# Moving the operand parts hh, hl, fh and fl to other residues in SBUF, in a two-part float32r matmul kernel

## The chip, the cores and the metric

The kernel runs on one core of one Trainium2 chip (trn2). The metric is the device time of one execution, in microseconds; the median of several executions is compared.

## The reference

The reference computes two transformer-like blocks on 256 positions of 1,024 features, batch 1. Cut to its matrix products:

```python
# first block
mod = silu(c) @ w_ada + b_ada                      # 6 modulation vectors
proj = (layer_norm(x) * (1 + sc1) + sh1) @ w_in    # 1024 -> 4096
ya = silu(layer_norm(causal_dwconv31(a_val * sigmoid(a_gate)))) @ w_pw_a
yb = einsum(pooled, w_pool) * pool_scale
x = layer_norm(ALPHA * x + g1 * ((sigmoid(gate_a) * ya + sigmoid(gate_b) * yb) @ w_out))
h = layer_norm(x) * (1 + sc2) + sh2
v, gt = split(causal_dwconv3(h @ w_up))            # 1024 -> 2 * 2816
x = layer_norm(ALPHA * x + g2 * ((gelu(gt) * v) @ w_down))
...
# second block, two layers: gated delta rule (w_in, w_out), SwiGLU (w13, w2),
#                           block attention (w_qkv, w_out), SwiGLU (w13, w2)
```

All of it is float32. The products with the large weights are more than nine tenths of the work.

## The kernel before, in words

The weights are cut into 311 units of 128 x 1,024 float32 (512 KB each), plus 48 units of `w_ada`, in the fixed order of a list, `PLAN`. SyncE's DMA queue loads them one after another into a ring `raw` of 11 slots. ScalarE rounds a unit to float32r into `hi` (line 1005, five slots), VectorE computes `lo = raw - hi` as float32r (line 1472, five slots), and the activations are split in the same way into `hh` and `hl` (8 chunks of 128 x 256 each) and, for the feed-forward stages, into `fh` and `fl` (4 chunks each). VectorE also does the 48 units of `w_ada` (line 1459).

TensorE then computes each product as three float32r matmuls, `hi*hh + hi*hl + lo*hh`, in the helper `three` (line 509), which nearly all matmuls go through. In `tile`, `first_tiles` and `rows_in` the weights' part is the stationary operand (128 columns) and the activations' part the moving one (256 columns); in `z` (the gate of the delta rule) and `rows_out_of` (the last feed-forward stage) the roles are exchanged, and the moving operand has 512 columns of weights. A matmul on the profile's page stands as `ps<-moving,stationary`: `ps<-hh,hi` streams `hh` past `hi`. Each matmul loads its stationary operand anew (a row of LDWEIGHTS), also where two in a row use the same one. Line 504 (`spin`) issues matmuls on a constant tile `idle` that no result uses. Lines 516 and 528 (`norm`) and line 607 (`conv`, the convolution over 31 positions) multiply plain float32; each of these stands as two records in the trace. `conv` reads its moving operand from `ypad` at element 2 + i for tap i, so from tap 12 on it starts 56, 60, 64, ... 128 bytes past a multiple of 128.

Each engine runs its own program in the order in which it is written; semaphores join them. The order of instructions and of waits is fixed in the source. SBUF tensors are placed one after another in the order of their `sb(...)` calls. Their first bytes in each partition are, in the build of before: `raw` 2,048, `hi` 47,104, `lo` 67,584, `hh` 88,064, `hl` 96,256, `fh` 104,448, `fl` 108,544, `idle` 112,640, `crow` 113,664, `xa` 117,760, `h` 125,952, `B0` 134,144 to `ev` 185,344, `Z` 189,440, `sm` 214,016, `blk` 215,040, `ones` 217,088: all of these are multiples of 1,024. `cst` starts at 218,624 and `vec` at 225,536 (both 512 past a multiple of 1,024), `mod` at 228,192. Within a unit, stationary tiles start every 512 bytes, and moving tiles of `hh` every 1,024.

Of the kernel before, what the change touches and what calls it, by code (L numbers as in the profile page):

```python
# [13 lines left out]
P = 128  # L14
# [277 lines left out]
def program(nc, wts, head, vecs, csts, rows, xtok, xT, low_dram, inv_dram, out):  # L292
    with ExitStack() as ctx:
        def sb(name, shape, dt=F):
            return ctx.enter_context(nc.sbuf_tensor(name, shape, dt))
# [2 lines left out]
            return ctx.enter_context(nc.semaphore(name))  # L298


        first = sb("first", [P, 184])
        dummy = sb("dumm", [P, 16])
        eps = sb("eps", [P, 24])
        raw = sb("raw", [P, RAW, 1024])
        hi = sb("hi", [P, SPLIT, 1024], FR)
        lo = sb("lo", [P, SPLIT, 1024], FR)
        hh = sb("hh", [P, NC, S], FR)
        hl = sb("hl", [P, NC, S], FR)
        fh = sb("fh", [P, 4, S], FR)
        fl = sb("fl", [P, 4, S], FR)  # L310
        idle = sb("idle", [P, S], FR)
# [7 lines left out]
        ypad = Z[:, 0:4 * 288].rearrange("p (g s) -> p g s", g=4)  # L319
        sm = sb("sm", [P, 256])  # L320
        blk = sb("blk", [64, 2, 256])
        ones = sb("ones", [P, 3, P])
        cst = sb("cst", [P, NCST])
        vec = sb("vec", [P, NVEC])
        mod = sb("mod", [P, 48])
        bank = [ctx.enter_context(nc.psum_tensor(f"ps{i}", [P, 512], F)) for i in range(8)]

        def V(name, i=0, n=1):
# [1872 lines left out]
```

## Time and profile before

| | |
|---|---|
| median of 3 runs | 1187.76 us (1185.19 to 1189.2) |
| the profiled execution, its own time | 1187.91 us |
| its span, first to last instruction | 1186.1 us |
| TensorE busy (matmuls) | 1129.2 us, 95% |
| VectorE busy | 808.1 us, 68% |
| ScalarE busy | 615.0 us, 52% |
| mean granted TensorE clock | 0.982 of full |
| moved by DMA | 195.60 MB, mean 165 GB/s |

The span lies 1.8 us below the execution's own time. Durations of matmuls in the rows contain the way through the array, and successive matmuls overlap, so the pace of TensorE is read from the starts in the timeline, not from the mean duration of one.

### The profile page before, as it was taken

The page shows a single profiled execution, that of the slowest core. Times are in us where ns is not written, and L with a number is a line of the kernel's source. Part 1 is how long each engine was busy: PE and PEld are TensorE (multiplying, and loading weights), DVE is VectorE, ACT ScalarE, POOL GpSimd, SP SyncE. Part 2 cuts the span into 40 slices and gives each one's busy share as a digit, 9 for nine tenths or more (in the row PEclk, how much of TensorE's full clock was granted, in tenths as well). Part 3 has the DMA queues.
Part 4 walks back from the last instruction along what each step waited for, and adds up shares of the span by engine and source line. Part 5 has one row for each costly group of instructions (what it writes and reads, how often), then busy time and mean ns, then how long its engine had stood idle before and what let it go on. Part 6 is the DMA issues. An engine that isn't in the chain of part 4 may idle for free.

```text
span 1186.1 us, 20553 instructions
## 1 busy us (share of the span) xinstructions
PE 1129.2 (95%) x8544; PEld 1090.4 (92%) x8544; DVE 808.1 (68%) x1360; ACT 615.0 (52%) x1028; POOL 3.3 (0%) x13
## 2 busy tenths in 40 slices
PE   7999989999999998879989999999999999999997
PEld 7998888899999997679989999999999799999996
DVE  7987479878877786585766755555589647555555
ACT  5567444556465548733443644444455545545453
POOL 0000000000000000000000000000000000000000
PEclk9999999999999998989989999999999999999999
DMA  9984237356766513133223265555435342655520
GB/s 376 419 313 160 72 142 273 100 183 227 243 209 205 187 65 122 46 100 140 90 72 125 90 197 192 178 182 177 159 116 193 120 141 82 220 193 180 187 80 36
DMA packets 58557, 195.60 MB, mean 165 GB/s; under 512 B 10848, under 2 KB 11232, under 8 KB 58208
## 3 DMA queue, kind: packets, MB, share of 16 engines
q1 hardware_dynamic: 58464, 194.28, 48.1%
q8 instruction: 68, 1.11, 0.4%
q14 instruction: 25, 0.20, 0.1%
HBM read 192.94 MB, written 1.31 MB: 164 GB/s over the span
## 4 chain that ended last, share of the span: by engine, by line
PE 76%; DVE 14%; ACT 6%; issue 2%; DMA 1%; SPq 1%; DVEq 0%; ACTq 0%
PE ps L509 64%; DVE lo L1472 3%; PE ps L722 3%; PE ps L516 2%; ACT hi L1005 2%; PE ps L607 2%; DVE raw L1459 1%; DVE B L1481 1%; PE ps L528 1%; DVE st L1489 1%; DVE B L1785 1%; DVE B L1494 1%; DVE ev L1710 1%; DVE B L1594 1%; SPq L477 1%
## 5 line engine op out<-in xcount | busy, mean ns | idle before, releaser
L509 PE MATMUL ps<-hh,hi 128*128 128x256 f32 x1792 | 515.9, 288 | 13.2 <-DVE hl L1506 3.4
L509 PE MATMUL ps<-hl,hi 128*128 128x256 f32 x1792 | 509.6, 284 | 0.0
L509 PE MATMUL ps<-hh,lo 128*128 128x256 f32 x1792 | 509.5, 284 | 0.0
L1472 DVE TENSOR_TENSOR lo<-raw,hi 128x1024 fp32r<-128x1024 f32 x311 | 378.2, 1222 | 179.3 <-ACT hi L1005 178.5
L509 PEld LDWEIGHTS ps<-hh,hi 128*128 128x128 f32 x1792 | 346.4, 193 | 16.9 <-issue 6.6
L1005 ACT ACTIVATE hi<-raw 128x1024 fp32r<-128x1024 f32 x311 | 324.0, 1050 | 55.8 <-PE ps L509 55.4
L509 PEld LDWEIGHTS ps<-hl,hi 128*128 128x128 f32 x1792 | 346.5, 193 | 1.0
L509 PEld LDWEIGHTS ps<-hh,lo 128*128 128x128 f32 x1792 | 346.3, 193 | 0.0
L509 PE MATMUL ps<-fh,hi 128*128 128x256 f32 x392 | 113.1, 289 | 4.0 <-ACT B L1109 2.7
L509 PE MATMUL ps<-fl,hi 128*128 128x256 f32 x392 | 112.1, 286 | 0.0
L509 PE MATMUL ps<-fh,lo 128*128 128x256 f32 x392 | 112.1, 286 | 0.0
L1166 ACT ACTIVATE ev<-ps 128x256 f32<-128x256 f32 x88 | 33.6, 382 | 132.9 <-PE ps L509 132.9
L509 PEld LDWEIGHTS ps<-fh,hi 128*128 128x128 f32 x392 | 76.4, 195 | 4.7 <-ACT B L1109 3.3
L509 PEld LDWEIGHTS ps<-fl,hi 128*128 128x128 f32 x392 | 76.6, 195 | 0.0
L509 PEld LDWEIGHTS ps<-fh,lo 128*128 128x128 f32 x392 | 76.5, 195 | 0.0
L1459 DVE CUSTOM_DVE_ANT_0 raw<-raw,crow 128x1024 f32<-128x1024 f32 x48 | 58.3, 1219 | 0.0
L504 PE MATMUL ps<-idle 128*128 128x256 f32 x404 | 55.3, 295 | 1.7 <-POOL Z L494 1.7
L1717 DVE TENSOR_TENSOR ev<-ev 128x256 f32<-128x256 f32 x66 | 28.1, 426 | 42.2 <-ACT ev L1166 31.5
L504 PEld LDWEIGHTS ps<-idle 128*128 128x128 f32 x404 | 51.9, 196 | 2.5 <-POOL Z L494 1.7
L1719 DVE TENSOR_TENSOR fl<-ev,fh 128x256 fp32r<-128x256 f32 x66 | 28.1, 425 | 31.9 <-ACT fh L1170 31.9
L1785 DVE SCALAR_TENSOR_TENSOR B<-ps,vec,B 128x255 f32<-128x255 f32 (+2 forms) x72 | 34.6, 481 | 22.0 <-ACT B L1255 20.3
L1170 ACT ACTIVATE fh<-ev 128x256 fp32r<-128x256 f32 x66 | 27.6, 418 | 35.9 <-DVE ev L1717 35.9
(256 smaller groups left out, 1223.7 us busy)
## 6 DMA issues: line engine op xcount, KB each, us to landing
raw<-in_w SPq DMA_DIRECT2D x359, 512.0 KB, 4.0
B<-in_t SPq DMA_DIRECT2D x2, 512.0 KB, 5.0
xa<-in_x SPq DMA_DIRECT2D x1, 1024.0 KB, 10.4
B<-in_r SPq DMA_DIRECT2D x1, 1024.0 KB, 6.2
out<-h SPq DMA_DIRECT2D x4, 256.0 KB, 2.0
cst<-in_c SPq DMA_DIRECT2D x1, 864.0 KB, 8.5
B<-between SPq DMA_DIRECT2D x32, 4.0 KB, 1.6
vec<-in_v SPq DMA_DIRECT2D x1, 328.5 KB, 6.7
```

The costliest lines, as they stand in the source:

```text
L504: g.matmul(bank[7][:, 0:S], idle[:, 0:P], idle[:, :], start=True, stop=True, skip_group_check=True)
L509: m = g.matmul(o, l, r, start=first and n == 0, stop=last and n == 2, skip_group_check=True)
L516: m = g.matmul(bank[bm][:, 0:S], ones[:, one, :], y[:, k, :], start=k == 0, stop=k == nch - 1, skip_group_check=True)
L722: m = g.matmul(bank[b][:, i * P:i * P + P], left(i), right(i), start=i == 0, stop=True, skip_group_check=True)
L1005: g.activation(hi[:, j % SPLIT, :], raw[:, PLACE[j] % RAW, :], ACT.Copy).then_inc(*up("hi", j))
L1166: g.activation(e, p, ACT.Copy if half else ACT.Silu).then_inc(*up("ff_out", (kup, t)))
L1170: g.activation(fh[:, j % 4, :], ev[:, (2 * j) % 4, :], ACT.Copy).then_inc(*up("f_hi", (kup, j)))
L1459: g.tensor_tensor_reduce(r, r, crow[:, :], 1.0, 0.0, ALU.mult, ALU.add, mod[:, col:col + 1]).then_inc(*up("ada", n))
L1472: g.tensor_tensor(lo[:, j % SPLIT, :], raw[:, PLACE[j] % RAW, :], hi[:, j % SPLIT, :].bitcast(F), ALU.subtract).then_inc(*up("lo", j))
L1717: g.tensor_tensor(e0, e0, e1, ALU.mult).then_inc(*up("f", (kup, j)))
L1719: g.tensor_tensor(fl[:, j % 4, :], e0, fh[:, j % 4, :].bitcast(F), ALU.subtract).then_inc(*up("f_lo", (kup, j)))
L1785: m = g.scalar_tensor_tensor(out=dst[:, d:], in0=bank[b][:, 0:S - d], scalar=V("a_conv", t * 4 + i), in1=dst[:, d:], op0=ALU.mult, op1=ALU ...
```

## The change

Only the places of SBUF tensors change. `mod` (192 bytes per partition) and `ones` (1,536 bytes) are allocated ahead of `hh` instead of at the end, an unused tensor `gap0` of 96 bytes follows them, and an unused `gap1` of 32 bytes stands between `hl` and `fh`.

```diff
         hi = sb("hi", [P, SPLIT, 1024], FR)
         lo = sb("lo", [P, SPLIT, 1024], FR)
+        mod = sb("mod", [P, 48])
+        ones = sb("ones", [P, 3, P])
+        gap0 = sb("gap0", [P, 24])
         hh = sb("hh", [P, NC, S], FR)
         hl = sb("hl", [P, NC, S], FR)
+        gap1 = sb("gap1", [P, 8])
         fh = sb("fh", [P, 4, S], FR)
         fl = sb("fl", [P, 4, S], FR)
         idle = sb("idle", [P, S], FR)
...
         blk = sb("blk", [64, 2, 256])
-        ones = sb("ones", [P, 3, P])
         cst = sb("cst", [P, NCST])
         vec = sb("vec", [P, NVEC])
-        mod = sb("mod", [P, 48])
```

In the build of the change, `raw`, `hi` and `lo` stay where they were. `mod` starts at 88,064, `ones` at 88,256 (64 bytes past a multiple of 128), `hh` at 89,888 and `hl` at 98,080 (both 32 past one), `fh` at 106,304 and `fl` at 110,400 (64 past one). Everything behind them up to `blk` moves up by 1,856 bytes and is then 64 past a multiple of 128: `idle` 114,496, `xa` 119,616, `B0` 136,000, `Z` 191,296 and so on. `cst` (218,944) and `vec` (225,856) move up by 320 bytes. No instruction is added, removed or moved on any engine, no wait changes, and every operand keeps its shape, type and strides.

## Rows read from the trace of the kernel before

**Rows 1.** The page: span, and busy time by engine.

```profile
span 1186.1 us, 20553 instructions
PE 1129.2 (95%) x8544; PEld 1090.4 (92%) x8544; DVE 808.1 (68%) x1360; ACT 615.0 (52%) x1028; POOL 3.3 (0%) x13
```

**Rows 2.** The page: the chain that ended last, by engine.

```profile
PE 76%; DVE 14%; ACT 6%; issue 2%; DMA 1%; SPq 1%; DVEq 0%; ACTq 0%
```

**Rows 3.** The chain from 640 to 910 us, one piece: start, us, what.

```profile
661.03 187.47 PE ps L509 x1560
```

**Rows 4.** Groups of matmuls (moving, stationary): count, busy us, mean ns, idle before.

```profile
L509 PE MATMUL ps<-hh,hi 128*128 128x256 f32 x1792 | 515.9, 288 | 13.2 <-DVE hl L1506 3.4
L509 PE MATMUL ps<-fh,hi 128*128 128x256 f32 x392 | 113.1, 289 | 4.0 <-ACT B L1109 2.7
L504 PE MATMUL ps<-idle 128*128 128x256 f32 x404 | 55.3, 295 | 1.7 <-POOL Z L494 1.7
L509 PE MATMUL ps<-hi,fh 128*128 128x512 f32 x88 | 34.5, 392 | 0.0
L509 PE MATMUL ps<-hi,hh 128*128 128x512 f32 x64 | 27.0, 422 | 0.0
```

**Rows 5.** Timeline of TensorE at full clock: start us, duration us, operands.

```profile
1019.57 0.28 PE L509 MATMUL ps<-hl,hi 128*128 128x256 f32 x1
...
1021.49 0.28 PE L509 MATMUL ps<-hh,lo 128*128 128x256 f32 x1
```

**Rows 6.** Timeline of TensorE at half clock, and that stretch's granted clock.

```profile
17.15 0.41 PE L509 MATMUL ps<-hl,hi 128*128 128x256 f32 x1
...
18.43 0.41 PE L509 MATMUL ps<-hl,hi 128*128 128x256 f32 x1
...
16.30:19.60 3.30, 2.80 (x13) 0.50 1.02 418
```

**Rows 7.** Timeline of TensorE: plain float32 of taps 12 and 14; one record's duration.

```profile
69.97 1.89 PE L607 MATMUL ps<-Z,B 128*128 128x256 f32 x8
79.18 1.89 PE L607 MATMUL ps<-Z,B 128*128 128x256 f32 x8
L607 PE MATMUL ps<-Z,B x152: 377/378/532, 70.0 to 139.2; 128*128 128x256 f32 x152
```

**Rows 8.** Timeline of TensorE: after a change of kind, and further on.

```profile
1008.21 0.40 PE L509 MATMUL ps<-hi,fh 128*128 128x512 f32 x1
1009.14 0.39 PE L509 MATMUL ps<-hi,fl 128*128 128x512 f32 x1
...
1010.96 0.28 PE L509 MATMUL ps<-hh,hi 128*128 128x256 f32 x1
1011.07 0.28 PE L509 MATMUL ps<-hl,hi 128*128 128x256 f32 x1
1171.55 0.39 PE L509 MATMUL ps<-lo,fh 128*128 128x512 f32 x1
...
1175.40 0.39 PE L509 MATMUL ps<-hi,fl 128*128 128x512 f32 x1
```

**Rows 9.** One tile's matmuls (hh): ns minimum, median, maximum.

```profile
L509 PE MATMUL ps<-hh,hi x1792: 277/283/562, 16.8 to 1169.4; 128*128 128x256 f32 x200
```

**Rows 10.** Groups of VectorE by form: shifted by 4 bytes, and in line.

```profile
L1594 DVE SCALAR_TENSOR_TENSOR B<-Z,vec,B 128x256 f32<-128x256 f32 x44 | 18.3, 478 | 0.0
L1530 DVE SCALAR_TENSOR_TENSOR xa<-ps,mod,B 128x256 f32<-128x256 f32 x16 | 6.4, 475 | 0.0
```

**Rows 11.** DMA issues: count, KB each, median us to landing.

```profile
raw<-in_w SPq DMA_DIRECT2D x359, 512.0 KB, 4.0
xa<-in_x SPq DMA_DIRECT2D x1, 1024.0 KB, 10.4
```

**Rows 12.** The chain from 210 to 420 us, shares by line.

```profile
by line: PE ps L509 63.1%; DVE lo L1472 10.6%; ACT hi L1005 3.9%; DVE raw L1459 3.8%; DVE ev L1710 3.3%; PE ps L516 2.9%; DVE ev L1707 2.7%; DVE B L1481 2.1%; issue 1.8%; DVE ev L1717 1.5%; ACT ev L1164 1.4%; DVE st L1489 0.8%; DVE h L1499 
```

**Rows 13.** Windows: us, busy us of VectorE, granted clock, DMA share, GB/s.

```profile
661.00:848.00 187.00, 103.43 (x124) 1.00 0.55 179
```

## The prediction

> **What bounds the kernel now.** I read the page's busy shares first. TensorE is at work in 95% of the span, VectorE in 68%, ScalarE in 52% [rows 1]. The chain of waits says the same of the end: three quarters of it are TensorE's [rows 2], and one piece of it is 1,560 matmuls of line 509 without a break, 187.47 us, or 120.2 ns each [rows 3]. So the time of this kernel is a number of matmuls times their pace, plus short serial stretches around the norms.
>
> The number comes from the groups. The three products with `hh` and `hl` moving are 1,792 each and the three with `fh` and `fl` 392 each: 6,552 matmuls of 256 columns; with the roles exchanged there are 3 x 88 + 3 x 64 = 456 of 512 columns [rows 4]. The 404 on `idle` fill waits and I leave them out. The clock was 0.982 of full in the mean; halved clock in 3.6% of the span is 43 us, or at most 200 matmuls. About 6,350 + 456 = 6,800 matmuls at full clock are left, so **each nanosecond per matmul is worth 6.8 us**, and 0.3% of the time, 3.6 us, is 0.5 ns per matmul.
>
> The pace comes from starts in the timeline. At full clock 16 successive matmuls take 1.92 us, 120.0 ns each [rows 5]. At half clock six take 1.28 us, 213.3 ns [rows 6]: that is 256 columns at 1.2 GHz and nothing else. At 2.4 GHz 256 columns are 106.7 ns, so 13.3 ns per matmul is something other than columns. Plain float32 does not have most of it: eight records of `conv` take 1.89 us from the first start to the last end, less 0.378 for the last one's duration, over seven, is 216 ns [rows 7], 2.7 over the 213.3 of its slower stream. With 512 columns the float32r matmul settles at 3.85 us for 17, 226.5 ns [rows 8], again 13.2 over 213.3. So the excess belongs to each float32r matmul with its load and not to its columns, and it is there only when the stream runs at the full rate. Its size is not fixed either: the first four of 512 columns after a change of kind take 0.93 us, 232.5 ns each, and the first of 256 behind them takes 0.11 us [rows 8]. The matmul's own duration goes from 277 ns to the usual 283 [rows 9]. This looks like the load of the next stationary operand and the moving stream getting in each other's way, in a rhythm that depends on how they stand in time. Whether it also depends on where they stand in memory is the whole question of this change.
>
> **The change part by part.** No instruction, wait or transfer is added or removed, so there is no term of the form "so many of these". Four things could have a price.
>
> 1. Moving operands 32 (`hh`, `hl`) or 64 (`fh`, `fl`) bytes past a multiple of 128, stationary ones unmoved: this touches all 6,800. In the trace of before every float32r operand starts at a multiple of 512, so no row varies what the change varies. Two things speak for zero. First, the pace is the same 120 whatever the distance of the two operands is in large steps: within a unit the weights' tile advances by 512 bytes and the moving tile by 1,024, through five slots, and the piece of rows 3 stays at 120.2 throughout. Second, the only operands that do vary in small steps cost nothing: tap 12 of `conv` reads its moving operand 56 bytes past a multiple of 128 and tap 14 64 past it, and eight records take 1.89 us both times [rows 7]. What weakens this: `conv` streams at half the rate and has none of the excess, so it has slack in which a collision would not be seen. Bounds: down to the 110 ns of the one fast start [rows 8], −10 ns; up to the 6 ns by which the slow starts of 512 columns lie over the settled pace. I take 0, since the nearest row with a small shift shows 0.
>
> The Trainium skill (TensorE: Matmul & The Clock Gate, Step-by-step: what each phase is for) says that TensorE has two independent SBUF read ports and that loading the next weights does not steal bandwidth from the running matmul. By that rule placement could not matter: this term would be 0, neither rival below would have a chance, and 3.6 us to both sides would do for the range. But the same page (Wait — 56ns, not 53.3ns?) gives a fixed 2.5 ns over the columns, where this trace has 13.3 for float32r and 2.7 for plain float32. The trace has room for a conflict of the two reads that the page excludes, so I keep both rivals.
>
> 2. Stationary `hh` and `fh`, moving `hi` and `lo` (456 matmuls, in `z` and `rows_out_of`): same question with the roles exchanged, already in the 6,800. Alone it would be worth at most 456 x 10 ns = 4.6 us.
>
> 3. VectorE and ScalarE operands 32 or 64 bytes off. The taps of line 1594, which read at 4-byte shifts, take 478 ns; line 1530, the same form on operands in line, takes 475 [rows 10]. Three nanoseconds on the 1,360 − 311 instructions that touch a moved tensor are 3.1 us, of which the chain carries 14%: 0.4 us. I take 0. The 311 of `lo` touch unmoved tensors alone.
>
> 4. Transfers. The 359 loads of weights go to unmoved slots; only a few land in moved tensors, such as `xa` in 10.4 us [rows 11]. They lie beside the weights' stream; the two of `in_t` at the start could delay the first norm. A fifth on a 5 us transfer is 1 us. I take 0.
>
> **The sum** is 1187.91 us, the profiled execution's own time (its span is 1186.1), plus 0. The median of the runs is 1187.76, 0.15 us lower, so I forecast 1187.8, with a range of its own of 3.6 us to both sides; 0.3% is also about the least that a measurement of this kernel can tell from no change.
>
> **The rivals.**
>
> *The excess shrinks* (the operands collided because both start on the same residue, and no longer do). For it: 13.3 ns is a large excess, it comes only with two full-rate reads, it varies by how they meet, and before, all three families of tensors stand on the same residue, after it on three different ones. Against it: rows 7. Price: what the excess loses. TensorE does not get all of it. In the first feed-forward stage, 210 to 420 us, only 63% of the chain is line 509 and the rest mostly VectorE's `lo` and `raw` [rows 12]; 210 us hold about 1,690 matmuls, and 37% of them, some 600, would gain nothing. Elsewhere there is room: in the piece of rows 3 VectorE is busy in 103 of 187 us [rows 13], so a pace of 110 leaves it under 61%. That leaves 6,200 matmuls. If half of the 10.6 ns over plain float32 goes, that is 5.3 x 6,200 = 33 us, 1155 us; if all, 66 us, 1122. The weights would still arrive: 24 matmuls at 110 ns are 2.64 us per 512 KB.
>
> *The excess grows*: the rhythm in which the pair has settled is a good one, and with the stream 32 bytes ahead of the load they meet as they do in the slow starts. It comes at each of the 6,800 matmuls, and nothing hides it, since TensorE is the bound. At the +6 ns of rows 8 that is 41 us, 1229 us. It decides from +0.5 ns per matmul on. Against it: the slow starts settle within four to six matmuls of themselves.
>
> That the change does not do what it says can be left out: the addresses of the build are 702 x 128 + 32 for `hh` and 830 x 128 + 64 for `fh`, and the instructions are the same.
>
> **How the numbers follow.** No change 0.42, because the only shifted rows show none; the excess shrinks 0.38, because something does collide and the change parts what stood on one residue; the excess grows 0.20, by the slow starts. The time is that of the first, 1187.8. The range must hold 8 times in 10, over both signs: from 1130, which leaves out the last part of a full gain (about 0.07), to 1203, which holds an excess grown by up to 2.2 ns and leaves out 0.12.
>
> **What the profile would show.** If I am right, the timeline has 120.0 ns between starts in every stage, and the long piece of the chain stays at 187 us. If the excess shrinks, starts stand 109 to 119 apart, the median duration of the `hh` matmuls falls from 283 towards 277, the piece of rows 3 falls below 185 us, and the first feed-forward stage gains the least. If it grows, starts of 256 columns stand 121 to 126 apart. A different pace for `fh` than for `hh` would say that the residue itself counts (64 against 32), a different pace with `hi` than with `lo` that the distance does. A changed VectorE or transfer time with the pace at 120 would make step 3 or 4 wrong.

## The result

The change is faster by 1.3%: 1170.92 us in the median of its four runs (1169.08 to 1176.3) against 1187.41, a ratio of 0.9869 with a 95% interval of 0.983 to 0.9909. The profiled execution took 1169.08 us with a span of 1167.3, 18.8 us below the span of before. So the forecast of no change was wrong; the time lies inside the range, on the side of the first rival.

The page after the change; line numbers are 3 higher than before, so line 512 is the helper `three`.

```profile
span 1167.3 us, 20553 instructions
PE 1109.0 (95%) x8544; PEld 1068.4 (92%) x8544; DVE 807.5 (69%) x1360; ACT 614.9 (53%) x1028; POOL 3.3 (0%) x13
...
PE 73%; DVE 17%; ACT 7%; issue 2%; SPq 1%; DMA 0%; POOL 0%; ACTq 0%; DVEq 0%; POOLq 0%
...
L512 PE MATMUL ps<-hh,hi 128*128 128x256 f32 x1792 | 511.2, 285 | 15.2 <-DVE hl L1509 3.5
...
L512 PE MATMUL ps<-fh,hi 128*128 128x256 f32 x392 | 109.9, 280 | 3.9 <-ACT B L1112 2.9
...
L507 PE MATMUL ps<-idle 128*128 128x256 f32 x404 | 55.3, 295 | 1.7 <-POOL Z L497 1.7
```

Against [rows 1] only TensorE's busy time has moved, by 20 us; VectorE and ScalarE are busy for as long as before. Within TensorE, the mean duration of the matmuls with `hh` and `fh` moving has fallen, 288 to 285 ns and 289 to 280, and that of `idle`, whose moving and stationary operand are the same tile, is 295 as before [rows 4].

The pace is in the timeline and in the long piece of the chain. Columns: start us, duration us, operands.

```profile
1011.10 0.28 PE L512 MATMUL ps<-hl,hi 128*128 128x256 f32 x1
...
1012.97 0.28 PE L512 MATMUL ps<-hh,lo 128*128 128x256 f32 x1
1155.66 0.39 PE L512 MATMUL ps<-hi,fh 128*128 128x512 f32 x1
...
1158.93 0.39 PE L512 MATMUL ps<-lo,fh 128*128 128x512 f32 x1
```

Sixteen matmuls of 256 columns take 1.87 us, 116.9 ns each, where [rows 5] had 120.0. Fourteen of 512 columns with exchanged roles take 3.27 us, 233.6 ns each, where [rows 8] settled at 226.5: these have become slower. The piece of 1,560 matmuls [rows 3] is here:

```profile
653.15 181.27 PE ps L512 x1560
```

It is 6.20 us shorter, 4.0 ns per matmul. I took the mean distance between starts over the whole trace as well, leaving out distances that hold a wait or a half-clock stretch: 117.04 ns for `hh` and `hl` (119.89 before, 5,224 and 5,250 matmuls), 115.42 for `fh` and `fl` (119.97, 1,155 and 1,134), 232.7 for 512 columns (228.9), 119.55 for `idle` (119.55). 5,224 x 2.85 = 14.9 us and 1,155 x 4.55 = 5.3 us less, 439 x 3.8 = 1.7 us more: the paces give 18.5 us, and the spans differ by 18.8.

That the two agree to 0.3 us is partly luck. The profiled execution after the change had 33.2 us of its span at half clock, the one before 43.5 (mean granted clocks 0.986 and 0.982). At 213.3 ns in place of 120 per matmul [rows 5, 6], 10.3 us less at half clock are worth up to 4.5 us, by my estimate. Against that, one stage kept only 2.0 us of what its pace would give, as shown below. The medians differ by 16.5 us.

### The profile page after: what moved, and what is told of

It is laid out like the page before. It is cut to its first block, busy times and chain, and to the rows that moved or that the text cites. A ratio compares the mean times of both kernels' runs of the same rounds, so it can differ in the third digit from the quotient of the medians.

```text
span 1167.3 us, 20553 instructions
## 1 busy us (share of the span) xinstructions
PE 1109.0 (95%) x8544; PEld 1068.4 (92%) x8544; DVE 807.5 (69%) x1360; ACT 614.9 (53%) x1028; POOL 3.3 (0%) x13
## 4 chain that ended last, share of the span: by engine, by line
PE 73%; DVE 17%; ACT 7%; issue 2%; SPq 1%; DMA 0%; POOL 0%; ACTq 0%; DVEq 0%; POOLq 0%
PE ps L512 61%; DVE lo L1475 4%; PE ps L725 3%; ACT hi L1008 2%; DVE raw L1462 2%; PE ps L610 2%; PE ps L519 2%; DVE B L1484 1%; PE ps L531 1%; DVE ev L1713 1%; DVE st L1492 1%; PE ps L507 1%; DVE ev L1710 1%; DVE B L1788 1%; DVE B L1497 1%
## 5 line engine op out<-in xcount | busy, mean ns | idle before, releaser
L512 PE MATMUL ps<-hh,lo 128*128 128x256 f32 x1792 | 504.3, 281 | 0.0
L512 PE MATMUL ps<-hl,hi 128*128 128x256 f32 x1792 | 503.9, 281 | 0.0
L512 PEld LDWEIGHTS ps<-hh,hi 128*128 128x128 f32 x1792 | 340.7, 190 | 19.9 <-issue 9.6
L512 PEld LDWEIGHTS ps<-hl,hi 128*128 128x128 f32 x1792 | 340.6, 190 | 1.1
L512 PEld LDWEIGHTS ps<-hh,lo 128*128 128x128 f32 x1792 | 340.7, 190 | 0.0
L512 PE MATMUL ps<-fh,hi 128*128 128x256 f32 x392 | 109.9, 280 | 3.9 <-ACT B L1112 2.9
L512 PE MATMUL ps<-fh,lo 128*128 128x256 f32 x392 | 108.8, 278 | 0.0
L512 PE MATMUL ps<-fl,hi 128*128 128x256 f32 x392 | 108.8, 277 | 0.0
L512 PEld LDWEIGHTS ps<-fl,hi 128*128 128x128 f32 x392 | 73.6, 188 | 0.0
```

The costliest lines, as they stand in the source:

```text
L512: m = g.matmul(o, l, r, start=first and n == 0, stop=last and n == 2, skip_group_check=True)
```

## The experiments

The theory after this result, called the pair theory below: the read of the moving operand and the load of the next stationary one collide, and how often depends on the distance of the two operands' addresses (the start of the moving one minus the start of the stationary one). The rivals: the moving operand's own residue counts, not the distance; or it was another moved tensor (`idle` and those behind it, most of which VectorE, ScalarE and the transfers use).

### One part of the change at a time

Only `hh` and `hl` 32 bytes past a multiple of 128 (h32_only):

```diff
+        gap0 = sb("gap0", [P, 8])
         hh = sb("hh", [P, NC, S], FR)
         hl = sb("hl", [P, NC, S], FR)
+        gap1 = sb("gap1", [P, 24])
         fh = sb("fh", [P, 4, S], FR)
```

> Only hh and hl move, to 32 bytes past a multiple of 128; fh, fl and everything behind are on multiples of 128. Pair theory: the 5,250 matmuls at full clock go from 119.9 to about 117.0 ns (less 15 us, a little of it lost where VectorE bounds), the 192 of 512 columns get 4 ns slower (plus 0.8 us): 1173 to 1175 us. If the tensors behind were the cause: 1187.

Measured: 1172.25 us, ratio 0.9864 (0.9847 to 0.9881): within 1 us of what was expected, and all of the gain of the change. `hh` runs at 116.81 ns. Unexpected: `fh`, at residue 0, runs at 118.62 and not at 120.

Only `fh` and `fl` at 64 (f64_only):

```diff
+        gap1 = sb("gap1", [P, 16])
         fh = sb("fh", [P, 4, S], FR)
         fl = sb("fl", [P, 4, S], FR)
+        gap2 = sb("gap2", [P, 16])
         idle = sb("idle", [P, S], FR)
```

> Only fh and fl move, to 64 bytes past a multiple of 128; everything behind them is back on multiples of 128. Pair theory: the 1,176 matmuls on them go from 120.0 to about 115.4 ns (less 5 us), the 264 of 512 columns from 228.8 to 232.4 (plus 1 us): 1183 to 1185 us. If the tensors behind were the cause: 1187.

Measured: 1188.94 us, ratio 0.9997 (0.9978 to 1.0016). A miss: `fh` came down only to 117.74 ns, not to the 115.4 that it has in the change, and the 512 columns went up to 233.7 ns, 4.9 more. 1,132 x 2.2 = 2.5 us less and 263 x 4.9 = 1.3 us more is a gain of 1.2 us, within what the runs can tell. So the pace of `fh` also depends on what `hh`, in the tiles between, leaves behind. The traces say more: `fh` at distance 64 has two paces. In the change it ran at 113.7 ns in the first SwiGLU of the second block and at 116.9 in the first feed-forward stage; in f64_only it ran at 117.9 in both. The pairs below show both, 113.3 and 117.8, at that distance.

Only what lies behind (behind_only):

```diff
         fl = sb("fl", [P, 4, S], FR)
+        gap2 = sb("gap2", [P, 16])
         idle = sb("idle", [P, S], FR)
```

> hh, hl, fh and fl stay; idle and everything behind it move to 64 bytes past a multiple of 128. Pair theory: nothing, 1187 us. If the operands of VectorE, ScalarE or the transfers were what counts: most of the 16 us of the change, 1171 us.

Measured: 1189.56 us, ratio 1.0009 (0.9996 to 1.0022). No pace moved (`hh` 119.89, `fh` 119.97 ns). The theory of another tensor falls.

The same piece of the chain in h32_only, f64_only and behind_only, in this order, one fence each:

```profile
651.59 183.27 PE ps L511 x1560
```
```profile
661.58 186.49 PE ps L511 x1560
```
```profile
660.48 187.48 PE ps L510 x1560
```

### The distance by itself

Three programs with nothing but matmuls on constants measure the pace of pairs of residues. Each was executed once. Below, 0/32 means the stationary operand 0 bytes in and the moving one 32. Each line is a run of 96 (or 48) in the order of `three` (the code is shortened):

```python
w(p, k, r) = wt[:, p * 4096 + k * 128 + r // 4 : ... + 128]   # stationary, r bytes in
m(q, k, r) = mv[:, q * 4096 + k * 256 + r // 4 : ... + 256]   # moving, r bytes in
[mm(bank[t][:, 0:S], w(p, k, a), m(q, k, b)) for t in range(4) for k in range(8) for p, q in THREE]
```

> A program that does none of the reference's work: constants in two tensors and, line by line, runs of 96 float32r matmuls of 256 columns (or 48 of 512) in the order of the helper three, each line with another pair of residues of the stationary and the moving operand; it copies x to the output. Pair theory (the excess depends on the residue of the moving operand relative to the stationary one): the pace of 256 columns is 120 ns at equal residues, also at 32/32 and 64/64, and about 117 and 115.5 at 0/32 and 0/64. Absolute theory (the moving operand's own residue counts): 32/32 gives 117 and 64/64 115.5, and moving the stationary operand alone does nothing. With 512 columns 226.7 at equal residues and about 233 at 32 or 64 apart.

In m1_pairs the lines went through one helper, so they are read by windows of 10 us, each within one line. Columns: window, its length and TensorE's busy us, matmuls that touch it (those under way at its start count too), granted clock, DMA. In this order (stationary/moving): 0/0, 0/4, 0/32, 0/64, 0/256, 64/0, 32/32, 64/64, 32/96.

```profile
24.00:34.00 10.00, 10.00 (x86) 1.00 0.01 2
36.00:46.00 10.00, 10.00 (x83) 1.00 0.01 2
70.00:80.00 10.00, 10.00 (x88) 1.00 0.01 2
92.00:102.00 10.00, 10.00 (x87) 1.00 0.01 2
183.00:193.00 10.00, 10.00 (x85) 1.00 0.01 2
240.00:250.00 10.00, 10.00 (x90) 1.00 0.00 0
274.00:284.00 10.00, 10.00 (x86) 1.00 0.01 2
286.00:296.00 10.00, 10.00 (x86) 1.00 0.00 0
319.00:329.00 10.00, 10.00 (x91) 1.00 0.01 2
```

By the starts, in the second half of each line: 0/0, 32/32, 64/64 and 0/256 exactly 120.0 ns; 0/4 123.3; 0/32 116.7; 0/64 117.8 (a miss, I expected 115.5); 64/0 and 32/96 113.3. With 512 columns 226.7 at 0/0, 32/32 and 64/64, and 233.4 at 32/0. The moving operand's own residue does not set the pace, since 32/32 and 64/64 are as 0/0: the absolute theory falls. The pair theory stands, with exceptions: 0/64 and 32/96 are both 64 apart and differ, and two more follow below.

> The same kind of program as m1_pairs, none of the reference's work: for each distance of 16 to 240 bytes of the moving operand from the stationary one, 96 matmuls of 256 columns behind 48 at distance 0, and again 96 behind 48 at distance 192. If the distance alone sets the pace: the same pace in both, with 113.3 ns at 112 and 192 as in m1_pairs. If the rhythm that was there before also counts (m1_pairs had 117.8 ns at 0/64 and 113.3 at 32/96, both 64 apart): two paces at some distances. If the pattern repeats after 128 bytes: 240 like 112 and 192 like 64. With 512 columns and the roles exchanged: 226.7 at 0 and 229 to 234 elsewhere.

In m2_residues each line is one group. Distances 16, 32, 64, 112, 128, 192 and 240 behind a run at distance 0 (columns: start, duration of the 96, line):

```profile
29.95 11.56 PE L67 MATMUL ps<-mv,wt 128*128 128x256 f32 x96
...
64.15 11.47 PE L71 MATMUL ps<-mv,wt 128*128 128x256 f32 x96
...
80.92 11.36 PE L73 MATMUL ps<-mv,wt 128*128 128x256 f32 x96
...
131.99 11.47 PE L79 MATMUL ps<-mv,wt 128*128 128x256 f32 x96
...
234.33 11.10 PE L91 MATMUL ps<-mv,wt 128*128 128x256 f32 x96
...
250.71 11.12 PE L93 MATMUL ps<-mv,wt 128*128 128x256 f32 x96
...
267.42 11.55 PE L95 MATMUL ps<-mv,wt 128*128 128x256 f32 x96
...
403.75 11.06 PE L111 MATMUL ps<-mv,wt 128*128 128x256 f32 x96
...
504.94 11.41 PE L123 MATMUL ps<-mv,wt 128*128 128x256 f32 x96
```

Lines 73 and 93 are distances 32 and 112 once more, behind a run at 192. Paces in the second half of each line (where there are two, the first is behind a run at 0, the second behind one at 192): 118.7 at 16 (116.7 in m1_pairs), 117.8 or 116.7 at 32, 118.3 at 48, 117.8 at 64, 120.1 or 118.4 at 80, 119.9 at 96, **113.3 at 112 in both**, 118.6 at 128, 118.8 or 118.6 at 144, 117.3 or 118.6 at 160, 119.2 at 176, 113.3 at 192, 119.1 at 208, 118.3 at 224, 117.1 at 240. So 240 is not as 112 and 128 not as 0: the pattern does not repeat after 128 bytes. 64 and 192 do not tell, since both have been seen at 113.3 and at 117.8. And some distances have two paces, by what ran before. The two runs of 48 at distance 192, one behind distance 16 and one behind 32:

```profile
41.35 5.82 PE L68 MATMUL ps<-mv,wt 128*128 128x256 f32 x48
...
75.47 5.62 PE L72 MATMUL ps<-mv,wt 128*128 128x256 f32 x48
```

The first settled at 117.8 ns, the second at 113.3, with nothing else different. With 512 columns and the stationary operand 176, 192 and 240 bytes in: 229.7, 228.9 and 226.7 ns, and 232.2 to 233.4 at the others of this program except 0 (in m1_pairs, 228.8 at 0/64, 230.7 at 8/0 and 234.3 at 96/0).

> None of the reference's work, as m1_pairs. (1) Pairs 112 bytes apart mod 256 (0/112, 0/368, 32/144, 64/176, 144/0 as stationary/moving): if the distance mod 256 sets the pace, 113.3 ns in the first four and in 0/1136 and 0/368, and 144/0 as well, since it is -144 = 112. (2) 72 matmuls on one and the same pair at distances 0 to 240: if the two reads of one matmul and the next load collide, the same distances matter as with changing operands; if it were the change of slots, 120 at every distance. (3) Plain float32, which streams at half the rate, at distances 0 to 192: if the excess is a collision of reads that needs the full rate, 216 ns per record at every distance.

Of m3_kinds three groups of 72 on one and the same pair at distances 0, 4 and 64 (lines 81, 82, 84), and three of plain float32, 48 records each, at distances 0, 4 and 112 (lines 89, 90, 93):

```profile
147.08 8.80 PE L81 MATMUL ps<-mv,wt 128*128 128x256 f32 x72
155.72 9.03 PE L82 MATMUL ps<-mv,wt 128*128 128x256 f32 x72
...
172.99 8.33 PE L84 MATMUL ps<-mv,wt 128*128 128x256 f32 x72
...
214.49 10.52 PE L89 MATMUL ps<-mv,wt 128*128 128x256 f32 x48
224.84 10.54 PE L90 MATMUL ps<-mv,wt 128*128 128x256 f32 x48
...
255.94 10.52 PE L93 MATMUL ps<-mv,wt 128*128 128x256 f32 x48
```

The same pair again and again has the same dependence (120.0, 123.4 and 113.3 ns), so the change of slots is not needed for it. Plain float32 has none: 216 ns per record at every distance. 0/112, 0/368, 0/1136, 32/144 and 64/176 all settled at 113.3, so whole multiples of 256 bytes do not count, nor does a common shift of 32 or 64. One miss: 144/0, which is -144 = 112 mod 256, settled at 118.3. Both lines below stand behind a run at 0/0, first 0/112, then 144/0:

```profile
29.90 11.10 PE L67 MATMUL ps<-mv,wt 128*128 128x256 f32 x96
...
79.96 11.52 PE L73 MATMUL ps<-mv,wt 128*128 128x256 f32 x96
```

m1_pairs has two more like it: 96/0 ran at 120.0 ns, where 0/160, the same distance mod 256, had 117.3 and 118.6, and 16/0 ran at 118.3, where 0/240 had 117.1. In all three the stationary operand is the one that is moved; 32/0, 64/0 and 128/0 agree with their distance. So the distance orders most pairs but is not all that counts. Whether these three are further rhythms of their distances, or the place of the stationary operand counts by itself, was not tried.

### The distances in the kernel

The same map, put into the kernel. All four tensors 4 bytes (1 element) in, which the pairs make slower (all4b), and 112 bytes (28 elements) in (all112):

```diff
-        hh = sb("hh", [P, NC, S], FR)
-        hl = sb("hl", [P, NC, S], FR)
-        fh = sb("fh", [P, 4, S], FR)
-        fl = sb("fl", [P, 4, S], FR)
+        hx = sb("hx", [P, 2 * NC * S + 64], FR)
+        fx = sb("fx", [P, 2 * 4 * S + 64], FR)
+        hh, hl = (hx[:, 28 + i * NC * S:28 + (i + 1) * NC * S].rearrange("p (c s) -> p c s", c=NC) for i in (0, 1))
+        fh, fl = (fx[:, 28 + i * 4 * S:28 + (i + 1) * 4 * S].rearrange("p (c s) -> p c s", c=4) for i in (0, 1))
```

> hh, hl, fh and fl 4 bytes past a multiple of 256, everything behind on multiples of 256. m1_pairs had 123.3 ns there, 3.3 above the 120 of equal residues: 3.3 ns x 6,350 = 21 us more, and 456 x 4 ns = 2 us: 1210 us, slower than before. If the misplacement of an operand only ever helps, or its lines do not matter: 1170 to 1188.

Measured: 1204.86 us, ratio 1.0135 (1.0114 to 1.0155), slower by 16 us; `hx` at 123.12 ns, `fx` at 123.24. The direction and the pace are as expected, the time is 5 us short of it. These executions had mean clocks of 0.982 to 0.985, those of before beside them 0.975 to 0.982. Over the 42 executions of before on record the time falls by some 0.74 us for each 0.001 of mean clock (a line through them, my estimate), so the clock may well be the missing 5 us.

> hh, hl, fh and fl 112 bytes past a multiple of 256 (a multiple of 16, not of 32), everything behind on multiples of 256. In m2_residues this distance went to 113.3 ns whatever ran before it, where 192 had two rhythms, 113.3 and 117.8. Pair theory: 6.6 ns x 5,800 = 38 us less and 456 x 5 ns = 2 us more: 1151 to 1155 us, with less spread between executions than all192 (1154 to 1170). If 112 is as unsteady in the real order: 1155 to 1170.

Measured: 1160.45 us, ratio 0.9766 (0.9749 to 0.9783), four runs within 1159.41 to 1161.8; `hx` at 114.16 ns, `fx` at 113.50. The pace is within 1 ns of the expected one, the time 5 to 9 us above, inside the range that was given for an unsteady 112. The pieces of the chain of all4b and all112:

```profile
669.39 192.66 PE ps L509 x1560
```
```profile
651.47 177.13 PE ps L509 x1560
```

Two more put all four tensors 192 or 64 bytes past a multiple of 256 with a `gap0` ahead of `hh` and the rest of 256 ahead of `idle`:

```diff
+        gap0 = sb("gap0", [P, 48])
         hh = sb("hh", [P, NC, S], FR)
...
+        gap2 = sb("gap2", [P, 16])
         idle = sb("idle", [P, S], FR)
```

> hh, hl, fh and fl 192 bytes past a multiple of 256, the weights' parts and everything behind on multiples of 256. Pair theory with the pace of m1_pairs at 192: 113.3 ns in place of 120 for the 6,400 matmuls of 256 columns at full clock, less 6.6 ns x 5,800 (some 600 gain nothing in the first feed-forward stage) = 38 us, plus 456 x 5 ns = 2 us: 1152 us. If the real order of slots and chunks does not settle in the fast rhythm: about 117 ns and 1171 us, as with the change.

> hh, hl, fh and fl 64 bytes past a multiple of 256. m1_pairs had 117.8 ns at 0/64 and 113.3 at 32/96, so between 1152 and 1176 us. If only the residue mod 128 counts, it is the same as with 192.

all192: 1167.36 us, ratio 0.9797 (0.9739 to 0.9855), with executions of 1154.41 to 1169.65; the profiled one, the fastest, had 114.38 ns. all64: 1176.94 us, ratio 0.9904 (0.9881 to 0.9926), `hh` at 117.40, as 0/64 had in m1_pairs. In these executions distance 64 gains less than 192.

To see whether 192 is unsteady and 112 is not, both once more:

> The kernel of all192 once more, for its spread (1154 to 1170 in four executions). If the spread is TensorE's granted clock, slower executions have a lower mean clock at the same pace of about 114.4 ns; if it is the second rhythm of distance 192, slower ones have a pace of up to 117.8 ns at the same clock. Median 1160 to 1168.

> The kernel of all112 once more, on the same chip as all192_again, to compare the two distances. The distance 112 has one rhythm only: 1158 to 1162 us again, faster than all192's median or the same as it within 0.3%.

all192: 1167.42 us, ratio 0.9813 (0.9792 to 0.9834), 1162.09 to 1169.68. all112: 1160.27 us, ratio 0.9751 (0.9736 to 0.9766), 1159.6 to 1161.25. The distance of 112 is faster: its executions lie at 1159.6 to 1161.25 us with clocks of 0.981 and 0.982, and the two of all192 at 0.980 and 0.981 took 1167.42 and 1164.26. It is also steadier, 2.4 and 1.7 us between the extremes of its two sets. The profiled execution of all192 had 114.85 ns and 1162.09 us.

Two things spread all192. In the second set the order by clock is nearly the order by time, from 1162.09 us at 0.983 to 1169.18 at 0.977. In the first set it isn't: 1154.41 us at 0.984, but 1165.27 at 0.987. The second rhythm is there too, and the two profiled executions show it. The same piece of 396 matmuls of the same kernel, in all192 and in all192_again:

```profile
841.55 46.54 PE ps L511 x396
```
```profile
846.25 48.26 PE ps L511 x396
```

By the starts, most of it runs at 113.3 ns in the first and at 117.8 in the second, the two rhythms that m2_residues has at distance 192, with nothing different in the program. The piece of 1,560 ran at the fast one in both. How much of the slower executions' time is this rhythm is open, since their traces were not kept. The two traces of all112 have no such difference: the same piece settled at 113.3 ns in both.

all112 is the best version that I ran: 29 us below before, some 10 us below the change.

## Why the prediction was wrong

**What bounds the kernel** held: a number of matmuls times their pace. In every kernel here the piece of 1,560 matmuls followed the pace, from 177.1 to 192.7 us.

**The excess** was read rightly: 13.3 ns per float32r matmul at full clock that belongs to no column, most of it absent in plain float32 (2.7 ns), and of no fixed size.

**Step 1 failed**: "I take 0, since the nearest row with a small shift shows 0". That row was `conv`, plain float32. I had written that it has slack in which a collision would not be seen, and took it as the nearest row all the same. m3_kinds shows that it could not have answered: plain float32 is at 216 ns at every distance, where float32r goes from 113.3 to 123.4 ns. The first argument, that the pace was the same whatever the distance in steps of 512 bytes, was true and empty, since multiples of 256 do not count. The bounds of the step, −10 and +6 ns, held all that was measured. So the term that was put at 0 came to −2.85 ns for `hh` and `hl` and −4.55 for `fh` and `fl`.

**Step 2** was right in that it was worth little. But I gave it no sign of its own, and it has the opposite one: the 456 matmuls with exchanged roles became 3.8 ns slower, 1.7 us in all.

**Steps 3 and 4** held: with only what lies behind `fl` moved the ratio was 1.0009 (0.9996 to 1.0022). The tap of `conv` and the line beside it, after the change, against [rows 10]:

```profile
L1597 DVE SCALAR_TENSOR_TENSOR B<-Z,vec,B 128x256 f32<-128x256 f32 x44 | 18.3, 477 | 0.0
L1533 DVE SCALAR_TENSOR_TENSOR xa<-ps,mod,B 128x256 f32<-128x256 f32 x16 | 6.4, 477 | 0.0
```

**The rival that the excess shrinks** is what happened, and I gave it 0.38. Its reason holds only in part: operands on one residue do have the 13.3 ns, but parting them is not enough, since 0/96 stayed at 120.0 ns and 0/4 went up to 123.3. Its signs came (starts 116.9 ns apart, the piece below 185 us, the median duration of the `hh` matmuls down from 283 to 280 ns, the first feed-forward stage gaining less than the one with the same matmuls). The sign for telling residue from distance was badly made: `fh` and `hh` did get different paces, yet by the pairs it is not the residue, and `hi` and `lo` start on the same residues, so they could not differ by distance. Its price of 5.3 ns was too high, 2.85 and 4.55 ns here. Its cut for the first feed-forward stage was too small: I let 37% of the matmuls there gain nothing, and counted 1,690 of them where the trace has 1,056 of `hh` and `hl` and 528 of `fh` and `fl`. Between the starts of the norms' matmuls ahead of the stage and behind it, it took 206.20 us before and 204.19 after, 2.0 us less, where 1,056 x 2.85 + 528 x 4.55 = 5.4 us were to be had: over 60% is lost. The chain of 206 to 410 us after the change, against [rows 12]:

```profile
by line: PE ps L512 44.0%; DVE lo L1475 18.4%; ACT hi L1008 6.6%; DVE raw L1462 6.1%; DVE ev L1713 5.7%; DVE ev L1710 4.8%; issue 2.8%; DVE ev L1720 2.6%; ACT ev L1167 2.5%; PE ps L519 1.8%; DVE B L1484 1.2%; DVE st L1492 0.8%; ACT B L1041 
```

Line 512 has gone from 63% to 44% of it, and VectorE's `lo`, `raw` and `ev` from 22% to 38%. TensorE's waits for `lo` there, in total, times and the longest, for before, the change and all112, one fence each:

```profile
PE ps L509 <- DVE lo L1472: 0.2, 1, 0.2
```
```profile
PE ps L512 <- DVE lo L1475: 2.2, 7, 0.7
```
```profile
PE ps L509 <- DVE lo L1472: 4.0, 9, 0.8
```

So the faster TensorE is, the more often it waits for VectorE's half of the split. I had named only `lo` and `raw`; what VectorE does there beside the split is above all the taps of the convolution over 3 positions, and much less the modulation's units (`raw`). VectorE's groups in 206 to 410 us after the change, their busy us, mean ns and idle time before:

```profile
L1713 DVE SCALAR_TENSOR_TENSOR ev<-ps,vec,ev 128x254 f32<-128x254 f32 x44 | 21.2, 482 | 1.6
L1710 DVE SCALAR_TENSOR_TENSOR ev<-ps,vec,ev 128x255 f32<-128x255 f32 x44 | 21.0, 478 | 3.6 <-ACT ev L1163 3.6
L1462 DVE CUSTOM_DVE_ANT_0 raw<-raw,crow 128x1024 f32<-128x1024 f32 x11 | 13.3, 1219 | 0.0
```

The stage with the same matmuls and neither of these two (the first SwiGLU of the second block) went from 203.93 to 197.75 us and kept its 6.2. Not all of the difference between the two stages is waiting: `fh` ran at 116.9 ns in the first and 113.7 in the second, the two rhythms again. In all112, where both ran at about 113.5 ns, the first gained 4.8 us and the second 10.3, where some 10 were to be had in each; this is the largest single part of what all112 lacks against its paces, though its expectation had already left out some 4 us for it. No run took the taps or the units away.

**The rival that it grows** exists, at another distance: 4 bytes, 3.2 ns, 16 us slower.

The Trainium skill (TensorE: Matmul & The Clock Gate, Step-by-step: what each phase is for) says that loading the next weights does not steal bandwidth from the running matmul. The float32r pairs are hard to square with that, 113.3 to 123.4 ns for the same work by the two addresses alone; the plain float32 ones, 216 ns everywhere, fit it. That the load is what costs the stream its time is still not shown, since no run left a load out. The Trainium skill (SBUF — State Buffer, Specifications (TRN2)) gives a price to each cross to a new 16-byte line. That could explain one more line at 4 bytes, but a start 8 bytes in also touches one more and settled at 120.0 in m1_pairs, and all multiples of 16 touch equally many and lie between 113.3 and about 120: the number of lines is not what counts.

## What to carry to other kernels

Where TensorE streams float32r at full rate with a load for each matmul, measure the distance between starts against columns over clock; if more than 2 or 3 ns are left, the distance of the moving and the stationary operand mod 256 bytes is worth a sweep, since equal residues cost 120.0 ns here and the best distance (112) 113.3. Keep the stationary operand where it is and move the other, as was done in the kernel, and sweep 512 columns by themselves: they were best at distance 0. Take several executions of each place, since some distances have two paces in one and the same kernel. A row that varies what a change varies is evidence only if it runs in the same regime: a row with slack that shows no effect bounds nothing. Count a faster pace only where the other engines have room, stage by stage, with the share of the chain that they take over. And before a sum of paces is held against two spans, compare their granted clocks: 0.004 of mean clock were some 10 us at half clock here.

## What the runs showed of the hardware that I had not expected

The pace of a float32r matmul of 256 columns depends on where its two operands stand to each other. The distance mod 256 bytes orders most pairs, and a common shift by 32 or 64 leaves 120.0 ns at 120.0; three pairs with only the stationary operand moved (16/0, 96/0, 144/0) do not follow it. It has more than one stable rhythm at some distances (113.3 and 117.8 ns at 192). In the pair programs what ran before picks it, and in the kernel the pace of `fh` changed with the place of `hh`, and two executions of all192 had different ones in the same stage. The excess over columns is 13.3 ns at distance 0 with 256 and with 512 columns alike; the best distance for 256 columns halves it to 6.6, and for 512 columns no distance tried was below that of 0 (226.7 ns). Why these distances and not others stays open: no model of a collision was tested, only the dependence of the pace on the two addresses, on the kind of number and on history.
